# Gated-delta sub-layers: half of the sample-state updates through ScalarE and GpSimd, a reordered recurrence, and transposes by a permuted identity

## What is computed

```
def step(S, xs):
    u_n, w_n, qg_n, attn_n, kdec_n, gl_n = xs
    v_new = u_n - w_n @ S
    o = qg_n @ S + attn_n @ v_new
    S = S * gl_n + kdec_n.T @ v_new
    return S, o
```

## Time and profile before

| | us |
|---|---|
| median of 3 runs | 2848.18 (2845.88 to 2850.45) |
| the profiled execution | 2844.36 |
| its span, first to last instruction | 2842.6 |
| mean granted TensorE clock | 0.964 of full |

### The profile page before, as it was taken

One profiled execution on the slowest core, in us unless ns is written; L12 is line 12 of the kernel. 1 busy time (PEld: TensorE's weight loads), 2 busy tenths in 40 slices (PEclk: granted clock), 3 DMA queues, 4 the chain that ended last, 5 costly groups with the idle time before them and its releaser, 6 DMA issues.

```text
span 2842.6 us, 51862 instructions
## 1 busy us (share of the span) xinstructions
PE 2703.2 (95%) x22064; PEld 2531.6 (89%) x22064; DVE 1556.6 (55%) x1998; ACT 1143.9 (40%) x1495; POOL 253.2 (9%) x278
## 2 busy tenths in 40 slices
PE   8998998899999999999999989999999989988998
PEld 7997887899999886699999978799999978878998
DVE  5546844655555445465465453465465468446554
ACT  4334442434444344344343332344343334424432
POOL 1000003100100124110010000010010000031000
PEclk9999999899999999999999999999999999988999
DMA  6544431444544635444445452444455444314443
GB/s 196 162 143 128 147 109 36 147 155 146 165 162 144 192 109 163 141 141 161 149 163 165 148 170 89 150 158 162 145 166 166 147 126 149 106 36 141 162 141 99
DMA packets 415625, 404.19 MB, mean 142 GB/s; under 512 B 14786, under 2 KB 411950, under 8 KB 415086
## 3 DMA queue, kind: packets, MB, share of 16 engines
q1 hardware_dynamic: 411348, 397.39, 44.2%
q0 software_dynamic: 4096, 4.20, 0.5%
HBM read 385.16 MB, written 16.39 MB: 141 GB/s over the span
## 4 chain that ended last, share of the span: by engine, by line
PE 88%; DVE 7%; ACT 2%; POOL 2%; issue 1%; DMA 0%; SPq 0%; DVEq 0%; POOLq 0%; ACTq 0%
PE psum L351 22%; PE psum L352 22%; PE psum L353 22%; POOL fbuf L406 1%; DVE x L537 1%; PE psum L2600 1%; DVE y L535 1%; PE psum L389 1%; PE psum L1177 1%; PE psum L1082 1%; PE psum L1099 1%; PE psum L968 1%; DVE xn_lo L470 1%; PE psum L1999 1%; PE psum L970 1%
## 5 line engine op out<-in xcount | busy, mean ns | idle before, releaser
L333 DVE TENSOR_TENSOR w_lo<-raw,w_hi 128x2048 fp32r<-128x2048 f32 (+3 forms) x366 | 752.3, 2055 | 556.0 <-ACT w_hi L326 555.9
L351 PE MATMUL psum<-xn_hi,w_hi 128*128 128x288 f32 x3296 | 987.1, 299 | 16.0 <-DVE w_lo L333 4.7
L352 PE MATMUL psum<-xn_lo,w_hi 128*128 128x288 f32 x3296 | 978.7, 297 | 0.0
L353 PE MATMUL psum<-xn_hi,w_lo 128*128 128x288 f32 x3296 | 975.0, 296 | 0.0
L326 ACT ACTIVATE w_hi<-raw 128x2048 fp32r<-128x2048 f32 (+3 forms) x366 | 624.3, 1706 | 787.7 <-PE psum L353 721.5
L351 PEld LDWEIGHTS psum<-xn_hi,w_hi 128*128 128x128 f32 x3296 | 623.8, 189 | 27.1 <-issue 15.3
L353 PEld LDWEIGHTS psum<-xn_hi,w_lo 128*128 128x128 f32 x3296 | 626.8, 190 | 0.0
L352 PEld LDWEIGHTS psum<-xn_lo,w_hi 128*128 128x128 f32 x3296 | 625.3, 190 | 0.4
L352 PE MATMUL psum<-h_lo,w_hi 128*128 128x288 f32 x1408 | 415.5, 295 | 0.0
L353 PE MATMUL psum<-h_hi,w_lo 128*128 128x288 f32 x1408 | 415.0, 295 | 0.0
L351 PE MATMUL psum<-h_hi,w_hi 128*128 128x288 f32 x1408 | 413.3, 294 | 0.0
(11 more groups left out here) (559 smaller groups left out, 3159.7 us busy)
## 6 DMA issues: line engine op xcount, KB each, us to landing
raw<-w_ffn_up SPq DMA_DIRECT2D x176, 1024.0 KB, 5.1
raw<-w_ffn_down SPq DMA_DIRECT2D x64, 768.0 KB, 4.5
raw<-w_ffn_down SPq DMA_DIRECT2D x64, 640.0 KB, 4.2
raw<-gdn_w_in SPq DMA_DIRECT2D x32, 1024.0 KB, 5.9
raw<-mlstm_w_in SPq DMA_DIRECT2D x12, 1024.0 KB, 5.4
raw<-gdn_w_out SPq DMA_DIRECT2D x8, 1024.0 KB, 6.9
raw<-cache_mla_latent SPq DMA_DIRECT2D x64, 128.0 KB, 2.2
a_split<-cache_mla_latent SPq DMA_DIRECT2D x64, 128.0 KB, 2.3
```

What stands on the lines that cost most here:

```text
L333: dve.tensor_tensor(wview(w_lo[slot(u, i)], u), wview(raw[u % NRAW], u), wview(w_hi[slot(u, i)], u).bitcast(F32), ALU.subtract).then_inc(l ...
L351: pe.matmul(out, wh[:, k, c], hi(k), start=st, stop=False)
L352: pe.matmul(out, wh[:, k, c], lo(k), start=False, stop=False)
L353: last = pe.matmul(out, wl[:, k, c], hi(k), start=False, stop=sp_)
```

## The change

* The odd steps of the sample update go another way: ScalarE copies bank 1 to one of two buffers in SBUF (`SSU`, which lie in `fbuf`), GpSimd adds the buffer to the state. The even steps stay on VectorE, in bank 0. A new semaphore `g_s_odd` counts GpSimd's adds, `g_ssu_copied` ScalarE's copies.
* On TensorE steps 4c and 4c+1 now stand after the q products, 4c+2 and 4c+3 after AY. On VectorE `updated` handles one step at a time, the first S copy comes ahead of mean 0, mean 1 comes in chunk 2 and not in chunk 1.
* The copies of AY for the first half of the prompt (L1676) move from VectorE to ScalarE.
* ScalarE's list is written out anew, with the copies between its other work.
* GpSimd's SE multiplies stand among the adds. Gated output 0 waits for the last add, since the buffers share memory with it.
* SP waits for VectorE's or GpSimd's count, by the head.
* Group 1's outputs are turned by four transposes with a permuted identity, cut from a constant table that grows by 64 columns.

```diff
-    base = [("ident", np.eye(P, dtype=np.float32)), ("ones", np.ones((P, P), np.float32))]
+    base = [("ident", np.eye(P, dtype=np.float32)), ("turn", np.eye(P, CH, dtype=np.float32)), ("ones", np.ones((P, P), np.float32))]
...
-        base = sb("base", [P, 2 * P])
-        ident, ones = base[:, 0:P], base[:, P:2 * P]
+        base = sb("base", [P, 2 * P + CH])
+        ident, swapped, ones = base[:, 0:P], base[:, CH:CH + P], base[:, P + CH:2 * P + CH]
...
+            SSU = [flat_f[:, 512 * q:512 * q + 512] for q in range(2)]
...
-                    once(sp, "g_s_new", 8 * (1 - g) + 5 + hh)
+                    once(sp, ("g_s_new", "g_s_odd")[hh % 2], 4 * (1 - g) + 3 + hh // 2)
...
-            for c in range(1, 4):
-                once(pool, "g_s", 2 * c)
-                for g in range(2):
-                    pool.tensor_tensor(SE[:, 4 * g:4 * g + 4, :], S[:, 4 * g:4 * g + 4, :],
-                                       EGL[:, c, 4 * g:4 * g + 4, None].to_broadcast([P, 4, P]), ALU.mult).then_inc(sem("g_se"), 1)
+            once(pool, "g_s0d", 8)
+
+            def added(k):
+                g, half, hh = 1 - k // 8, k // 4 % 2, k % 4
+                once(pool, "g_ssu_copied", k // 2 + 1)
+                v = S0[4 * g + hh][:, 4 * half:4 * half + 4, :]
+                pool.tensor_tensor(v, v, SSU[k // 2 % 2].rearrange("q (b e) -> q b e", b=4), ALU.add).then_inc(sem("g_s_odd"), 1)
+            for c in range(4):
+                if c > 0:
+                    added(4 * c + 1)
+                if c < 3:
+                    once(pool, "g_s", 2 * c + 2)
+                    for g in range(2):
+                        pool.tensor_tensor(SE[:, 4 * g:4 * g + 4, :], S[:, 4 * g:4 * g + 4, :],
+                                           EGL[:, c + 1, 4 * g:4 * g + 4, None].to_broadcast([P, 4, P]), ALU.mult
+                                           ).then_inc(sem("g_se"), 1)
+                if c == 0:
+                    added(1)
+                added(4 * c + 3)
...
-            once(pe, "g_s_new", 16)
+            once(pe, "g_s_new", 8)
+            once(pe, "g_s_odd", 8)
...
-                    once(pe, "g_s_new", k - 1)
+                    once(pe, ("g_s_new", "g_ssu_copied")[k % 2], k // 2)
...
-                sample_update(pe, range(4 * c, 4 * c + 1))
+                sample_update(pe, range(4 * c, 4 * c + 2))
...
                 once(pe, "g_o", 2)
+                once(pe, "g_ay_copied", 2)
...
-            sample_update(pe, range(4 * c + (c > 0), 4 * c + 4))
+            sample_update(pe, range(4 * c + 2 * (c > 0), 4 * c + 4))
...
-                    if g == 0:
-                        last = pe.transpose(psum[:, OBANK[k], hh * P:(hh + 1) * P], O[:, g, p, hh, :], ident)
-                        continue
-                    for e in range(2):
-                        c = hh * P + e * CH
-                        last = pe.matmul(psum[:, OBANK[k], c:c + CH], O[:, g, p, hh, :],
-                                         ident[:, halves(1 - e)], start=True, stop=True)
+                    last = pe.transpose(psum[:, OBANK[k], hh * P:(hh + 1) * P], O[:, g, p, hh, :], (ident, swapped)[g])
...
-            once(act, "g_su", 2)
-            act.activation(S[:, 4:8, :].rearrange("q h e -> q (h e)"), psum[:, SUBANK[1], :], ACT.Copy).then_inc(sem("g_s"), 1)
-            once(act, "g_s_o", 1)
-            for g in range(2):
-                last = square(Os[:, g, :], 16 + g, junk[:, g, :])
-            last.then_inc(sem("g_ms"), 1)
-            root(0, slice(16, 18))
-            for g in range(2):
-                act.activation(Os[:, g, :], Os[:, g, :], ACT.Copy, scale=RO[:, 16 + g:17 + g]).then_inc(sem("g_on"), 1)
-            for p in range(2):
+            def update_copied(k):
+                once(act, "g_ssu", k + 1)
+                if k > 4:
+                    once(act, "g_s_odd", k // 2 - 1)
+                act.activation(SSU[k // 2 % 2], psum[:, 1, :], ACT.Copy).then_inc(sem("g_ssu_copied"), 1)
+
+            def q_scaled(p):
                 for g in range(2):
                     once(act, "g_qs", 2 * p + g + 1)
                     for hh in range(4):
...
                         last = act.activation(O[rows, g, p, hh, :], psum[rows, QSBANK[g], hh * P:(hh + 1) * P], ACT.Copy,
                                               scale=CE[rows, 3, c:c + 1])
                     last.then_inc(sem("g_qe"), 1)
-                for g in range(2 - p):
-                    once(act, "g_o", 2 * p + g + 1)
-                    for hh in range(4):
-                        last = square(O[:, g, p, hh, :], 8 * p + 4 * g + hh, junk[:, 4 * g + hh, :])
-                    last.then_inc(sem("g_ms"), 1)
-                root(1 + p, slice(8 * p, 8 * p + 8))
-                for g in range(2 - p):
-                    for hh in range(4):
-                        c = 8 * p + 4 * g + hh
-                        last = act.activation(O[:, g, p, hh, :], O[:, g, p, hh, :], ACT.Copy, scale=RO[:, c:c + 1])
-                    last.then_inc(sem("g_on"), 1)
+
+            def squared(p, g):
+                once(act, "g_o", 2 * p + g + 1)
+                if p == 0:
+                    once(act, "g_ay_copied", g + 1)
+                for hh in range(4):
+                    last = square(O[:, g, p, hh, :], 8 * p + 4 * g + hh, junk[:, 4 * g + hh, :])
+                last.then_inc(sem("g_ms"), 1)
+
+            def normed(p, g):
+                for hh in range(4):
+                    c = 8 * p + 4 * g + hh
+                    last = act.activation(O[:, g, p, hh, :], O[:, g, p, hh, :], ACT.Copy, scale=RO[:, c:c + 1])
+                last.then_inc(sem("g_on"), 1)
+            once(act, "g_su", 2)
+            act.activation(S[:, 4:8, :].rearrange("q h e -> q (h e)"), psum[:, SUBANK[1], :], ACT.Copy).then_inc(sem("g_s"), 1)
+            once(act, "g_s_o", 1)
+            for g in range(2):
+                last = square(Os[:, g, :], 16 + g, junk[:, g, :])
+            last.then_inc(sem("g_ms"), 1)
+            update_copied(1)
+            root(0, slice(16, 18))
+            for g in range(2):
+                act.activation(Os[:, g, :], Os[:, g, :], ACT.Copy, scale=RO[:, 16 + g:17 + g]).then_inc(sem("g_on"), 1)
+            update_copied(3)
+            q_scaled(0)
+            update_copied(5)
+            for g in range(2):
+                once(act, "g_ay", g + 1)
+                act.activation(O[halves(g), g, 0].rearrange("q h e -> q (h e)"), psum[halves(g), AYBANK[g], :], ACT.Copy
+                               ).then_inc(sem("g_ay_copied"), 1)
+            update_copied(7)
+            squared(0, 0)
+            update_copied(9)
+            squared(0, 1)
+            update_copied(11)
+            root(1, slice(0, 8))
+            normed(0, 0)
+            normed(0, 1)
+            q_scaled(1)
+            update_copied(13)
+            update_copied(15)
+            squared(1, 0)
+            root(2, slice(8, 16))
+            normed(1, 0)
...
-            def updated(ks):
-                for k in ks:
-                    g, half, hh = 1 - k // 8, k // 4 % 2, k % 4
-                    once(dve, "g_ssu", k + 1)
-                    once(dve, "g_s0d", 4 * (1 - g) + hh + 1)
-                    v = S0[4 * g + hh][:, 4 * half:4 * half + 4, :]
-                    dve.tensor_tensor(v, v, psum[:, k % 2, :].rearrange("q (b e) -> q b e", b=4), ALU.add
-                                      ).then_inc(sem("g_s_new"), 1)
+            def updated(k):
+                g, half, hh = 1 - k // 8, k // 4 % 2, k % 4
+                once(dve, "g_ssu", k + 1)
+                once(dve, "g_s0d", 4 * (1 - g) + hh + 1)
+                v = S0[4 * g + hh][:, 4 * half:4 * half + 4, :]
+                dve.tensor_tensor(v, v, psum[:, 0, :].rearrange("q (b e) -> q b e", b=4), ALU.add).then_inc(sem("g_s_new"), 1)
...
-            mean(0, slice(16, 18))
...
-                    updated(range(4 * c, 4 * c + 1))
+                    updated(4 * c)
...
+                if c == 0:
+                    updated(0)
+                    mean(0, slice(16, 18))
...
-                        if p == 0:
-                            dve.tensor_copy(O[halves(g), g, p], four(psum[halves(g), AYBANK[g], :]))
...
-                updated(range(4 * c + (c > 0), 4 * c + 4))
-                if c == 1:
+                updated(4 * c + 2)
+                if c == 2:
                     mean(1, slice(0, 8))
             once(dve, "g_ro", 3)
...
+            once(dve, "g_s_odd", 8)
```

4 lines of the change are left out of this document (2 added, 2 removed).

## The result

| | before | after |
|---|---|---|
| median | 2847.95 (2845.88 to 2850.45, 4 runs) | 2817.69 (2812.93 to 2820.37, 4 runs) |
| the profiled execution | 2844.36 | 2812.93 |
| its span | 2842.6 | 2811.2 |
| mean granted TensorE clock | 0.964 | 0.970 |

The ratio is 0.9892 with an interval of 0.9874 to 0.9909: faster by 30.3 us, where 27.1 had been forecast. The two profiled executions lie 31.4 us apart.

A forecast was written before the change was run, and what follows sets the result against it. Only the gated-delta stretches, 101.45 us, could give time, through TensorE's waits and low clock. Savings of 14.9 and 16.5 us, 31.4 together, less 4.3 for the clock gave 27.1, so 2821; own case 2817 to 2826, 50%.

The forecast's parts named there:

- TensorE's cycle, 6.1 us: Recurrence from chunk 3 on, at full clock: state products, two update pairs, L1206 and L1214 sum to 6.1 us per chunk.
- Chunk 0: Before chunk 1: an earlier S copy on VectorE lets chunk 1 start near 468.6, not 469.29, saving 0.7 us.
- Chunks 1 and 2: Odd updates wait for ScalarE's copies, update 7 tightest, yet chunk 2 starts at 474.7 and chunk 3 at 480.8.
- GpSimd: GpSimd's odd-update adds and SE multiplies: an add priced at 1.02 us, bounds 0.69 and 2.04, hidden either way.
- Chunk 3: Last chunk: ScalarE binds and the change loses time, 10.2 us from chunk 3's start to mean 2, before 8.1.
- Tail: Mean 2 to the projection's first matmul, L351: VectorE is the bound, 7.6 us, before 13.42.
- four-pass bound: Group 1's output transposes: permuted identity costs at most four times L1232's 0.22, making output 5 1.0 us late per layer.
- Stores: State stores before the second projection unit: out by 498.3, unit ready by 503.1, needed at 505; hidden by 2 us.
- The clock charge: Recurrence: 4.3 us charged in both layers for one 3.4 us half-clock stretch per layer and update 15 sometimes slow.
- the clock full throughout: Rival: the denser recurrence holds TensorE's clock, saving 31.4 us and up to 3 more, 2813 to 2817; 17%.
- The clock low as before: Rival: recurrence at low clock for 10.2 and 13.7 us, 2829, or nearly throughout, 2836 to 2841; 23%.
- The slower rival, GpSimd's queue: Rival: GpSimd's multiplies and adds delay gated 0 once an add takes 4.5 us; at 5 us, 2855; 3%.

The follow-up runs named there:

- e7: e4 with updates 2 and 3 behind chunk 1's q products, 4 and 5 behind its state product, removing the idle spell before chunk 1: 2808.88 us, ratio 0.9871.
- e5: The changed kernel with a second, useless GpSimd add of the same size ahead of each odd add: 2819.77 us, ratio 0.991.
- e4: The changed kernel with ScalarE's list reordered around chunk 3 and mean 1 ahead of update 10's add on VectorE: 2813.9 us, ratio 0.988.
- e1: The kernel before with only the permuted-identity transposes and their constant table added: 2838.12 us, ratio 0.9967.
- e8: The changed kernel with TensorE's old order of updates, one after the q products and three after AY, offload kept: 2827.13 us, ratio 0.9932.
- e9: e3 with group 1's outputs turned by the old half-width matmuls, leaving only the reordered recurrence: 2817.83 us, ratio 0.9895.
- e3: The changed kernel with all update adds on VectorE, no ScalarE copies or GpSimd adds, and mean 1 placed earlier: 2815.99 us, ratio 0.9883.
- e10: e3 with e7's order of updates, all adds on VectorE: 2811.02 us, ratio 0.987.

## Why the prediction was right, point by point

Forecast 2821, measured 2817.7; the profiled execution was forecast at 2817.3 and took 2812.93. That execution was 4.4 us off, 3.2 of it in the two stages and 1.1 outside them. The median is only 3.3 off by luck: it stands 4.8 above the profiled execution and not the 3.8 taken over from the kernel before. It lies at the lower edge of the forecast's own case, 2817 to 2826.

1. *TensorE's cycle, 6.1 us.* It measured 6.12 or 6.13 in three of four chunks of the change, and in the fourth the clock was low. Pairs cost what one update costs.
2. *Chunk 0.* Forecast 5.1 from the first state product to chunk 1, measured 5.25. The idle spell was named (466.8, measured 0.86 us at 467.79), and e7 shows what it costs: 0.87 in itself, and in layer 0 1.6 by the clock.
3. *Chunks 1 and 2.* No wait of TensorE at updates 7 and 11. That ScalarE might bind earlier did not come about.
4. *GpSimd.* **Mis-sized:** an add was priced at 1.02 us, half of the SE pair in the earlier trace rows, and took 1.27. It lay between the bounds and was hidden all the same. e5 doubled the work for 1.3 us per layer. The step that the prediction lacked is what GpSimd does to VectorE beside it; in the change that fell on mean 1 (0.75 for 0.17) and on a square (1.55 for 0.69). The square ended no wait of the chain. Mean 1 did: ScalarE's root waited for it, and everything in chunk 3 up to mean 2 hangs on that root.
5. *Chunk 3.* ScalarE binds, forecast 10.2 to mean 2, measured 10.01. Two misses cancel in this: the 0.6 that mean 1 was held is in no term of the sum, and the rest took 0.8 less than its terms. Counted from chunk 3's start (482.81, forecast 480.8; 1.6 of the difference is chunk 1's clock) copy 15 ends at 8.8 where 8.7 was forecast; the squares behind it took 1.2, not 1.4. e4 took the delay away by ScalarE's order and mean 1's place and got 8.11.
6. *Tail.* Forecast 7.6, measured 7.28. The transposes cost what L1232 did (e1), so the four-pass bound fell.
7. *Stores*. The last update ended 10.8 us after chunk 3's start, forecast 10.9. ScalarE split the second unit at 499.92, straight after its last high part, and VectorE had it ready at 504.2; TensorE waits for nothing between L351 and 520. Hidden, as forecast.
8. *The clock charge.* **This term was too large.** It took 4.3 off the saving: 1.7 per layer for a stretch after the idle spell and 0.45 per layer for a slow update 15. The profile shows one such stretch, 1.6 us in layer 0 (7.74 against 6.13), none in layer 3, and update 15 at full clock both times (1.09). Against the stages that gives 30.3 saved where 31.4 - 4.3 = 27.1 had been forecast: the 3 us by which the forecast missed. The stages differ from the forecasts with full clock (35.0 each) by +1.4 and -0.2. (The sum has 6.3 for chunk 1, where 12.3 to 6.1 is 6.2; its own steps add up to 35.1.)

Of the rivals, the clock full throughout would have given 2813 to 2817, and the measured median stands 0.7 above that; the profiled execution shows it in layer 3 and not in layer 0. The clock low as before did not happen in the change. e8, which brings waits back, also brings back 9 us at 0.50; but the waits aren't the whole condition, since chunk 1 of e9's layer 3 ran at 0.57 without any. The slower rival, GpSimd's queue, needed an add of 4.5 us; with the double adds of e5, 1.04 + 1.27 = 2.3, nothing had yet piled up.

What the prediction did not ask is how its 31 us divide. It summed chunks and tail, which was right, but spoke of the offload as part of the 6.1 us cycle: "each odd update now waits for ScalarE's copy". The runs show that the cycle needs only the order. The order alone gives the whole gain (e9), the transposes alone 9.4 us, transposes and offload with the old order about 19, and the offload on top of the order nothing measurable (e3 against the change, e10 against e7). In the change that is because the copies and the held mean 1 delay ScalarE in chunk 3 by about what the offload saves elsewhere; in e7, where chunk 3 is as short as e10's, because it gives back behind mean 2 most of what it saves in chunk 1.

## What to carry to other kernels

When side work stands in TensorE's list ahead of a serial chain, first place it in pairs where its buffers are free, with VectorE's list in the same order; here that gave the whole gain, with two copies moved to ScalarE as the only work on another engine. A handoff to another engine has to be charged with what it delays in that engine's own list and in VectorE's beside GpSimd (together 1.8 us per layer in chunk 3) and is worth a run without it. Parts of a change that shorten the same wait don't add, so each should be timed alone and left out.
